# First loads of the attention stage in another order: the first gate ahead, the decode tile's loads ten units later, queries and keys fourteen units ahead, the bias table in two large pieces

## What is computed

```python
h = rmsnorm(x) * (1 + scale) + shift              # shift, scale, gate from c
p = split(h @ w_in)                               # 4932 columns
# branch A: an indexer scores all keys, each query keeps its best 256 (or L/4)
logits = q . ks * HEAD_DIM**-0.5 + rel_bias[t5_bucket(sel_pos - q_pos)]
att_a  = softmax(logits) @ vs                     # 8 heads on 2 kv heads
# branch B: sliding window of 3 chunks of 64, sinks, the same bias table
att_b  = softmax_with_sink(q . k * HEAD_DIM**-0.5 + bias) @ v
o_a = (att_a * silu(z_a)) @ w_oa ; o_b = (att_b * silu(z_b)) @ w_ob
y = x + gate * ((sigmoid(g_a) * o_a + sigmoid(g_b) * o_b) @ w_out)
```

## Time and profile before

| | us |
|---|---|
| median of 3 runs | 1013.48 (1010.45 to 1014.51) |
| the profiled execution, its own time | 1018.09 |
| span of its trace | 1016.3 |
| PE busy | 959.4 (94%) |
| DVE busy | 652.5 |
| ACT busy | 392.3 |
| POOL busy | 375.1 |

### The profile page before, as it was taken

How to read it: one execution, slowest core, us unless ns; L and a number is a source line. 1 busy time by engine, 2 the same in 40 slices (tenths; PEclk the granted TensorE clock), 3 DMA queues, 4 the chain that set the end, 5 groups by cost and what they waited for, 6 DMA issues and landing times. The chain is left out here.

```text
span 1016.3 us, 17645 instructions
## 1 busy us (share of the span) xinstructions
PE 959.4 (94%) x6482; PEld 855.6 (84%) x6482; DVE 652.5 (64%) x1375; ACT 392.3 (39%) x1166; POOL 375.1 (37%) x420
## 2 busy tenths in 40 slices
PE   4859999999999999999999888999999889999998
PEld 2558887878789999999999666778777679999998
DVE  6563365999999999999980575766665553331111
ACT  5664566444422322122111555666665522212100
POOL 0261113212253533121243477655631145537332
PEclk9878999999999999999999798999999899999999
DMA  9820013643461323232132834423334665534332
GB/s 319 305 73 28 25 34 108 227 162 94 141 205 59 115 82 108 81 107 76 63 136 71 252 97 139 140 91 102 96 102 111 196 189 163 152 93 139 101 121 73
DMA packets 112187, 126.40 MB, mean 124 GB/s; under 512 B 12105, under 2 KB 89305, under 8 KB 111978
## 3 DMA queue, kind: packets, MB, share of 16 engines
q1 hardware_dynamic: 101698, 114.30, 36.2%
q10 hardware_dynamic: 10408, 11.01, 3.5%
HBM read 95.49 MB, written 35.75 MB: 129 GB/s over the span
## 5 line engine op out<-in xcount | busy, mean ns | idle before, releaser
L1569 PE MATMUL PS<-HH,WH 128*128 128x384 f32 (+1 forms) x576 | 188.8, 328 | 0.0
L1571 PE MATMUL PS<-HH,WL 128*128 128x384 f32 (+1 forms) x576 | 187.9, 326 | 0.0
L1570 PE MATMUL PS<-HL,WH 128*128 128x384 f32 (+1 forms) x576 | 187.7, 326 | 0.0
L1404 DVE MAX8 M<-SC 128x8 f32<-128x384 f32 (+3 forms) x210 | 174.8, 870 | 11.6 <-DVE SC L1409 11.0
L1409 DVE MATCH_REPLACE8 SC<-M,SC 128x384 f32<-128x384 f32 (+3 forms) x210 | 179.9, 864 | 0.0
L880 POOL TENSOR_TENSOR WL<-RAW,WH 128x512 fp32r<-128x512 f32 x72 | 94.2, 1312 | 182.0 <-ACT WH L1031 182.0
L1569 PE MATMUL PS<-WH,HH 128*128 128x512 f32 (+3 forms) x288 | 111.1, 386 | 8.6 <-DVE HL L1348 8.5
L1569 PEld LDWEIGHTS PS<-HH,WH 128*128 128x128 f32 x576 | 108.1, 188 | 3.8 <-issue 3.7
L1570 PE MATMUL PS<-WL,HH 128*128 128x512 f32 (+3 forms) x288 | 109.0, 378 | 0.0
L1571 PE MATMUL PS<-WH,HL 128*128 128x512 f32 (+3 forms) x288 | 108.7, 377 | 0.0
L1570 PEld LDWEIGHTS PS<-HL,WH 128*128 128x128 f32 x576 | 108.1, 188 | 0.0
(11 more groups left out here) (202 smaller groups left out, 1967.4 us busy)
## 6 DMA issues: line engine op xcount, KB each, us to landing
RAW<-in_w_all SPq DMA_DIRECT2D x72, 256.0 KB, 2.7
gz<-STG SPq DMA_DIRECT2D x48, 192.0 KB, 1.8
WADA<-in_w_ada SPq DMA_DIRECT2D x16, 512.0 KB, 12.3
snat<-STG SPq DMA_DIRECT2D x24, 256.0 KB, 2.0
QKV<-snat SPq DMA_DIRECT2D x8, 768.0 KB, 5.7
GT<-gz SPq DMA_DIRECT2D x32, 192.0 KB, 2.5
XN<-in_x_prompt SPq DMA_DIRECT2D x8, 512.0 KB, 6.1
btad<-bvd ACTq DMA_DIRECT2D x4, 1024.0 KB
```

Of the source, the lines that this page charges most:

```text
L1404: V.max(M8[0:r, a, :], w).then_inc(sel_step, 1)
L1569: T.matmul(out, wh, mh, start=first, stop=False)
L1570: T.matmul(out, wh, ml, start=False, stop=False)
L1571: return T.matmul(out, wl, mh, start=False, stop=last)
```

## The change

Five edits. The gate of group 0 is loaded at step -1 in place of 4. BTA 768 to 1023 and VA are issued at step 1 of SP's loop, the six loads of the decode tile at step 9. QKV is loaded 14 units ahead of its tile's base in place of 7. The six pieces of BTA become two, on ACT's queue: columns 512 to 767 (1 MB, rows of 1 KB) at step 13 and columns 0 to 511 (2 MB, rows of 2 KB) at step 36; DVE waits for them at steps 32 and 64.

```diff
-        LOAD_AT, NORM_AT, SPLIT_AT = -7, -5, 2
+        LOAD_AT, NORM_AT, SPLIT_AT = -14, -5, 2
-        BT_AT = {13 if tt == 2 else 16 * (tt - 1) + 3: tt for tt in range(2, SAMPLE)}
-        ZT_AT = {GEND[g] + (2 if g == 2 * NT - 1 else 0 if g // 2 == SAMPLE else -4): g for g in range(2 * NT)}
+        ZT_AT = {GEND[g] + (2 if g == 2 * NT - 1 else 0 if g // 2 == SAMPLE else -9 if g == 0 else -4): g for g in range(2 * NT)}
...
             sp.dma_start(BTB[:], btbd).then_inc(kvb_in, 16)
             sp.dma_start(VB[:], vp[:, :, 1408:1536]).then_inc(kvb_in, 16)
-            sp.dma_start(BTA[:, :, 768:1024], btad[:, :, 768:1024]).then_inc(kvc_in, 16)
-            sp.dma_start(VA[:], vp[:, :, 640:768]).then_inc(kvc_in, 16)
-            for dst, src in ((CK[:, 0:4, :], ...), ...):
-                sp.dma_start(dst, src).then_inc(rest_in, 16)
             for i in range(3):
                 sp.wait_ge(stg_out[i], 16 * NST[i])
...
-                if s in BT_AT:
-                    tt = BT_AT[s]
-                    if tt >= 3:
-                        sp.wait_ge(min_done, 16 * (tt - 1) + 1)
-                    sp.dma_start(BTA[:, :, 896 - 128 * tt:1024 - 128 * tt], btad[:, :, 896 - 128 * tt:1024 - 128 * tt]).then_inc(bta_in, 16)
+                if s == 1:
+                    sp.dma_start(BTA[:, :, 768:1024], btad[:, :, 768:1024]).then_inc(kvc_in, 16)
+                    sp.dma_start(VA[:], vp[:, :, 640:768]).then_inc(kvc_in, 16)
+                if s == 9:
+                    for dst, src in ((CK[:, 0:4, :], ...), ...):
+                        sp.dma_start(dst, src).then_inc(rest_in, 16)
...
             # ScalarE's loop
+                if s in (13, 36):
+                    c = slice(512, 768) if s == 13 else slice(0, 512)
+                    if s == 36:
+                        act.wait_ge(min_done, 33)
+                    nc.scalar.dma_start(BTA[:, :, c], btad[:, :, c]).then_inc(bta_in, 16)
...
             # VectorE's loop
-                if s % 16 == 0 and 32 <= s < U8:
-                    dve.wait_ge(bta_in, 16 * (s // 16 - 1))
+                if s in (32, 64):
+                    dve.wait_ge(bta_in, 16 * (s // 32))
```

More of the change, by code:

```diff
@@ L750, in _ @@
                     g_load(0)
-                if s in BT_AT:
-                    tt = BT_AT[s]
-                    if tt >= 3:
-                        sp.wait_ge(min_done, 16 * (tt - 1) + 1)
-                    sp.dma_start(BTA[:, :, 896 - 128 * tt:1024 - 128 * tt], btad[:, :, 896 - 128 * tt:1024 - 128 * tt]).then_inc(bta_in, 16)
+                if s == 1:
+                    sp.dma_start(BTA[:, :, 768:1024], btad[:, :, 768:1024]).then_inc(kvc_in, 16)
+                    sp.dma_start(VA[:], vp[:, :, 640:768]).then_inc(kvc_in, 16)
+                if s == 9:
+                    for dst, src in ((CK[:, 0:4, :], t["cache_ak"].rearrange("(n p) c -> p n c", p=128)), (CK[:, 4, :], t["cache_bk"]),
+                                     (VAS[:, 0:4, :], t["cache_av"].rearrange("(n p) c -> p n c", p=128)),
+                                     (VAS[0:DEC, 4, :], snat[SEQ:TOK, 640:768]),
+                                     (VBS[:, 0, :], t["cache_bv"]), (VBS[0:DEC, 1, :], snat[SEQ:TOK, 1408:1536])):
+                        sp.dma_start(dst, src).then_inc(rest_in, 16)
                 tt = prep(s, LOAD_AT)
```

## The result

| | before | changed |
|---|---|---|
| median, us | 1013.05 (1009.87 to 1017.64, 7 runs) | 1019.15 (1016.1 to 1023.96, 7 runs) |
| ratio | | 1.0074, 95% interval 1.0046 to 1.0103 |
| profiled execution, its own time | 1018.09 | 1023.0 |
| its span | 1016.3 | 1021.2 |

The change makes the kernel 0.7% slower, by about 7 us. The prediction said 1011.3, with 1006.5 to 1015.5 as range, and was wrong.

A forecast was written before the change was run, and what follows sets the result against it. PE, busy 959.4 of 1016.3 us, was taken to wait at tile 3 on a chain of small transfers begun by a late QKV. 1.4 + 1.5 - 0.8 + 0.1 = 2.2 us off 1013.5 gave 1011.3, range 1006.5 to 1015.5.

The forecast's parts named there:

- BTA in two pieces on ACT's queue: Steps 13 and 36: SP's saved issues worth 0, ACT's issues covered; RB of group 0 delayed 0, at most 1.7 us.
- Rival C: Group 3 to tile 4: RB waits for the whole 2 MB piece; 1015.8, or 1018.8 with a clock fall; chance 0.11.
- C's room: Tile 4: 3.4 us at PE, 1.2 ahead of KSC, less PE's 2.2 gain; a delay matters from 2.4 us on.
- The round robin: DMA engines alternate between queues with work, so RB of group 3 shares: 1.7 in place of 0.9 us, under 2.4.
- Tile 2's QKV ahead of the caches: First loads: QKV lands about 577.6 in place of 580.23, so POOL's product for group 0 starts 1.4 us earlier.
- DVE's stall: Group 1: DVE's sum no longer meets XNB on POOL; PE's 1.58 us wait goes, but PE keeps only 1.4 us.
- Tile 3's QKV: Moved behind group 0's store: 1.5 us gained at group 1's store to attd, 0.8 us lost at its rdd.
- The sum of 2.2 us: Whole gain, seen at tile 3: PE waits about 1.7 in place of 2.49 us and goes on at 616.2.
- The first gate: Gate of group 0 loaded first: worth 0, hidden by DVE's cast; it pushes BTA and VA back by 0.9 us.
- the later caches: Cache loads ten units later, landing about 580 and wanted at step 32: cost 0, cover some 25 us.
- rival A: Low-clock stretches behind 586 and 617 us vanish: gain 5.2 us, 1008.3, or 1007 if tile 3's wait shrinks; chance 0.22.

The follow-up runs named there:

- With small pieces: Changed kernel with the six 512 KB pieces of BTA back on SP's queue at their old steps, other four edits kept: 0.9988 (0.9973 to 1.0003).
- second profile of before: The kernel before, unchanged, profiled once more; its own time was 1010.82 us.
- the kernel with only the caches later: Kernel before with the first gate in front and BTA, VA and the caches later, QKV 7 units ahead as before: 0.9997 (0.9984 to 1.0011).

## Why the prediction was wrong

- **The step that failed** is "BTA in two pieces on ACT's queue", and in it "for RB0 I take 0; the bound is 1.7 us". RB of group 0 took 6.8 us to land in place of 2.9, 3.9 more, and the 1 MB piece alone cost 3.5 us. The reasoning weighed only the second 512 KB, at the mean rate of 302 GB/s, and took it that a piece beside is no worse than one ahead. RB took 4.7 us behind 1 MB on one queue and 6.8 beside it. The whole 1 MB at that rate is 3.5 us, so even a bound by all its bytes was too low; on two queues the small load waited nearly as long as the large one took (8.1 us).
- **Rival C was the case**, and I gave it 0.11. Its place, its chain and its point were right: the 2 MB piece, group 3, PE's wait ahead of tile 4, a delay of over 2.4 us. Its size was dismissed by the sentence that RB's 256 KB "then take 1.7 in place of 0.9 us". What stood beside the 2 MB piece was not RB but the rdd store that comes before it, behind QKV, a key store and a gate on SP's queue; its landing went from 3.2 to 8.9 us, 5.7 more, where a small piece behind the same QKV gave 2.5 more. I named RB alone and left out what the change itself had put in front of it.
- **C's room** was misjudged as well. The 3.4 us at PE came from the first profile; in the second KS of tile 4 is done at 637.42 and PE comes at 638.58, 1.2 us of room, and QKV 14 units ahead leaves 0.1, with small pieces. The 2.4 us also took off PE's gain of 2.2 us, by which the chain would have come earlier too. That C's 1018.8, with the clock, lies near the measured 1019.15 is in part luck: it holds nothing for tile 2, where PE waited 1.91 us.
- **The round robin.** "DMA: Bandwidth & Descriptors" of the Trainium skill has each DMA engine go round robin between queues that have work. Both queues did move data at once, as it says, but 0.60 MB in 294 packets against 0.11 MB in 158 in two microseconds. Taking turns was no equal share of bytes, and I had read it as one.
- **Tile 2's QKV ahead of the caches** went right: expected near 577.6, XG began at 576.02, on a time axis that runs 1.4 us ahead of that of before at this point, so at 577.4 by the old axis. What XG waited for last was the landing of a key store. With small pieces group 0's product came 1.3 us earlier against the first transposes of KS (22.1 and 23.4), the 1.4 of the sum. In the changed kernel RB took it, and more.
- **DVE's stall**: no XNB met DVE's sum in the changed kernel, and PE's 1.58 us wait is not there, as said. But it isn't there in the second profile of before either, where XNB ended at 584.19 and the sum began at 585.02, so its absence is no work of the change. In the changed kernel it wasn't on the path either, since PE then waited for POOL.
- **Tile 3's QKV**: group 1's store landed in 2.3 us (SP's gate load came 2.3 us behind it, 600.36 and 602.66) as taken. But the 1.5 us were not there to be gained: with QKV at its old place the store lands in 2.4 us in the second profile of before, and in 2.3 in the kernel with only the caches later. What made it 3.8 us in the first profile stays open. The rdd of group 1 took 3.2 in place of 2.6 us, 0.6 lost of the 0.8 taken (4.0 us and 1.4 lost with small pieces), and the gate ahead of it 3.4 in place of 2.8. The loss of 2.5 us at the rdd of group 3, which QKV brings together with a small piece, had no term. Measured alone, the QKV edit comes to 1.0003, nothing.
- **The headroom.** The sum of 2.2 us was to shorten a wait of 2.49 us. In the second profile of before that wait is 1.02 us. My prediction noted that the profiled execution was 4.6 us over the median and then put the whole gain on the median; a chain that binds by 2.5 us in a slow instance binds by 1.0 in one of 1010.82 us, itself 2.2 under the median, and by 1.17 in the kernel with only the caches later, profiled at 1012.75. Small pieces brought 1.2, with an interval that holds nothing.
- **The first gate, the later caches**: nothing, as said.
- **The clock** (rival A): in the changed kernel it stayed up behind tile 3 and fell behind tile 4 instead, from the new wait on. That the low clock added to the loss there is read from one execution, not shown by a comparison of its own.

## What to carry to other kernels

Before a transfer is made larger, moved ahead or put on another queue, list the small transfers that someone waits for while it is in flight, in the order of the queue, and price each as if it waited for all of the large one. If the chain has less room than that, keep the pieces small or move the large one to where a tile is longer: 2 MB were free 14 steps later. And when the profiled execution is slower than the median, its waits are not the waits of the median: profile again before a gain is counted from one of them.

## What the hardware showed that I had not expected

- A 4 KB store took 8.9 us to land with QKV's 768 KB and 2 MB in flight, the 2 MB on either queue, where it took 5.7 behind QKV and a 512 KB piece and 3.2 behind that piece without QKV. Two loads of 128 KB took 6.8 us beside 1 MB on the other queue but 4.7 behind it on their own. A second queue did not shield the small transfers; for RB it was worse.
- Issuing is not always 0.6 us: of four transfers of 512 KB in a row the last three held ACT for 5.8 us, and its arithmetic with it. A queue on a computing engine can stop that engine; the same 2 MB as one transfer with rows of 2 KB were issued in 0.54 us.
- Two profiles of the same kernel, 1018.09 and 1010.82 us, differ by 4.0 us in the 110 us from the first transposes of KS to group 8.
